# Hybrid decoder step: gate and up projections as seven block products over three token groups

## What is computed

```
x  = x + concat(A, B) @ w_out                       # output projection, 1024 -> 1024
h2 = RMSNorm(x)
g, u = split(h2 @ w_ffn_in)                         # 1024 -> 2 x 2816
gc = conv_b + conv over 3 tokens of g               # per column
x  = x + (silu(gc) * u) @ w_down                    # 2816 -> 1024
```

## Time and profile before

| | us |
|---|---|
| median of three runs | 2675.08 |
| lowest and highest run | 2668.12, 2677.18 |
| span of the profiled execution (first to last instruction) | 2668.3 |
| TensorE matmul busy | 2510.4 (94%) |
| TensorE weight load busy | 2220.7 (83%) |
| VectorE busy | 1310.5 (49%) |
| ScalarE busy | 739.9 (28%) |
| GpSimd busy | 207.2 (8%) |
| mean granted TensorE clock | 0.964 of 2.4 GHz |

### The profile page before, as it was taken

The page is one execution under the profiler, slowest core; times in us unless marked ns, Lnnn a source line. Parts: engine busy times, 40 slices in busy tenths (PEclk is TensorE's granted clock), DMA queues, the critical chain, the costliest instruction groups (busy, mean ns, idle before and its releaser), DMA issues.

```text
span 2668.3 us, 36833 instructions
## 1 busy us (share of the span) xinstructions
PE 2510.4 (94%) x13536; PEld 2220.7 (83%) x13536; DVE 1310.5 (49%) x2357; ACT 739.9 (28%) x1460; POOL 207.2 (8%) x234
## 2 busy tenths in 40 slices
PE   5999978999996799689999999999999999999998
PEld 4888857999994687578888888888999999999997
DVE  3666634666665444234444444444444444444444
ACT  2444423333331222132222222221322222222221
POOL 2223210222221000000000000000000000000000
PEclk9999968999996899899999999999999999999999
DMA  7222202111111567641111111114611111111111
GB/s 272 91 103 83 81 15 80 60 50 52 55 36 26 188 212 258 203 134 48 53 49 47 47 47 47 47 51 164 199 40 41 46 47 47 45 42 39 47 32 71
DMA packets 189315, 219.87 MB, mean 82 GB/s; under 512 B 20310, under 2 KB 152742, under 8 KB 187180
## 3 DMA queue, kind: packets, MB, share of 16 engines
q1 hardware_dynamic: 188928, 218.84, 25.1%
q10 hardware_dynamic: 288, 0.07, 0.0%
q0 software_dynamic: 32, 0.07, 0.0%
HBM read 156.77 MB, written 63.13 MB: 82 GB/s over the span
## 4 chain that ended last, share of the span: by engine, by line
PE 57%; DVE 0%; DMA 0%; issue 0%; ACT 0%; SPq 0%; DVEq 0%
PE ffn_bank L109 19%; PE ffn_bank L111 19%; PE ffn_bank L110 19%; DMA ffn_stage<-in_w_ffn_in_dram 0%; DVE ffn_stage L2383 0%; PE ffn_bank L2167 0%; DVE ffn_w_lo L2337 0%; DVE ffn_w_lo L2266 0%; ACT ffn_w_hi L2229 0%; DVE ffn_raw L2314 0%; SPq L2066 0%; DVEq L1978 0%; DVEq L77 0%
## 5 line engine op out<-in xcount | busy, mean ns | idle before, releaser
L109 PE MATMUL ffn_bank<-late_h,ffn_w_hi 128*128 128x512 f32 (+2 forms) x1760 | 619.4, 352 | 18.5 <-DVE ffn_w_lo L2337 16.5
L111 PE MATMUL ffn_bank<-late_h,ffn_w_lo 128*128 128x512 f32 (+2 forms) x1760 | 619.0, 352 | 0.0
L110 PE MATMUL ffn_bank<-late_h,ffn_w_hi 128*128 128x512 f32 (+2 forms) x1760 | 618.8, 352 | 0.0
L109 PEld LDWEIGHTS ffn_bank<-late_h,ffn_w_hi 128*128 128x128 f32 x1760 | 331.1, 188 | 47.7 <-DVE ffn_w_lo L2337 16.7
L2329 DVE TENSOR_TENSOR ffn_acc<-ffn_bank,ffn_acc 128x512 f32<-128x512 f32 (+1 forms) x374 | 257.9, 690 | 203.8 <-PE ffn_bank L111 203.8
L110 PEld LDWEIGHTS ffn_bank<-late_h,ffn_w_hi 128*128 128x128 f32 x1760 | 331.1, 188 | 28.1
L111 PEld LDWEIGHTS ffn_bank<-late_h,ffn_w_lo 128*128 128x128 f32 x1760 | 330.9, 188 | 27.8
L2303 DVE SCALAR_TENSOR_TENSOR ffn_t<-ffn_gp,ffn_cc,ffn_t 128x512 f32<-128x512 f32 (+2 forms) x220 | 142.0, 645 | 342.3 <-ACT ffn_t L2208 338.4
L109 PE MATMUL ffn_bank<-ffn_d_hi,ffn_act_hi 128*128 128x512 f32 (+1 forms) x748 | 291.4, 390 | 4.0 <-issue 4.0
L110 PE MATMUL ffn_bank<-ffn_d_lo,ffn_act_hi 128*128 128x512 f32 (+1 forms) x748 | 291.3, 389 | 0.0
L111 PE MATMUL ffn_bank<-ffn_d_hi,ffn_act_lo 128*128 128x512 f32 (+1 forms) x748 | 291.1, 389 | 0.0
(11 more groups left out here) (302 smaller groups left out, 3590.0 us busy)
## 6 DMA issues: line engine op xcount, KB each, us to landing
ffn_stage<-in_w_ffn_in_dram SPq DMA_DIRECT2D x88, 512.0 KB, 3.8
ffn_stage<-in_w_down_dram SPq DMA_DIRECT2D x44, 512.0 KB, 3.4
ml_hh<-h_parts SPq DMA_DIRECT2D x16, 1024.0 KB, 4.8
att_x<-in_x_prompt_dram SPq DMA_DIRECT2D x16, 512.0 KB, 3.5
h_parts<-att_h_hi SPq DMA_DIRECT2D x16, 512.0 KB, 2.7
h_parts<-att_h_lo SPq DMA_DIRECT2D x16, 512.0 KB, 3.4
out_o<-mixed SPq DMA_DIRECT2D x16, 512.0 KB, 5.6
out_x<-in_x_prompt_dram SPq DMA_DIRECT2D x16, 512.0 KB, 3.9
```

The source lines that it names most:

```text
L109: nc.tensor.matmul(out, a_hi, b_hi, start=first, stop=False)
L110: nc.tensor.matmul(out, a_hi, b_lo, start=False, stop=False)
L111: return nc.tensor.matmul(out, a_lo, b_hi, start=False, stop=last)
```

## The change

h2 is stored once, in fp32, and not split in `output`. `ffn` has three groups: 768, 768 and 576 tokens (the last 64 are the sample). A group's h2 is cut in four blocks: model width in halves, tokens in halves (384, 384, 288 tokens). Gate (u = 0) and up (u = 1) of the two chunks of a round are one 2x2 block product each, done with seven block products where the plain way has eight. For these, four sums of h2 blocks are made per group (three on VectorE, one on GpSimd) and four sums of weight blocks per round and unit, on GpSimd. A block product is 4 pieces times 3 matmuls of 384 (288) columns; a unit is 84 matmuls. Three banks take the seven products; ScalarE copies two of them out, VectorE adds the others in five `combine` steps. A round is now: unit 0, the down projection of the round before, unit 1. The product silu(gate)·up moves to GpSimd (`gate`), the small copies of the convolution too. The rounds are written out, with no hardware loop. Weight loads are 1 MB each, three a round. Core of the diff:

```diff
@@ output
-            def store_h(t):
-                h_split.wait(sp, t)
-                for part, src in ((0, h_hi), (1, h_lo)):
-                    h_out.mark(sp.dma_start(h2_dram[:, part, ...
+            def store_h(t):
+                h_kept.wait(sp, t)
+                h_out.mark(sp.dma_start(h2_dram[:, 0, :, bass.ds(t.n * P, r)], cut(h_t[:, t.p, :], r)), t)
...
+        def load_first(sp, q):
+            part, half = ((0, 0), (1, 0), (1, 1), (0, 1))[q]
+            ops.load_a(sp, h2_dram, GROUPS[0], part, half)
+            if q == 0:
+                ops.load_b(sp, ins["w_ffn_in"][0], 0, 0)
@@ ffn
-GROUPS = (Group(0, 0, [(0, 512), (512, 512)], False), Group(1, SEQ // 2, [(0, 384), (384, 384), (768, 320)], True))
+GROUPS = (Group(0, 0, 768, False), Group(1, 768, 768, False), Group(2, 1536, 576, True))
+PRODUCTS = ((A11, B11, 0), (S2, T2, 1), (A12, B21, 0), (S3, T3, 1), (S1, T1, 2), (A22, T4, 1), (S4, B22, 2))
+PIECE_OF = (0, 1, 0, 2, 3, 2, 3)
...
+            def unit(G, i, u):          # TensorE
+                before = (i - 1, 5 + 3, 5 + 4, 3) if u == 0 else (i, 3, 4, 1)
+                for n, (a, b, bk) in enumerate(PRODUCTS):
+                    w_split(pe, G, i, 4 * u + PIECE_OF[n])
+                    if n == 0:
+                        w_cact(pe, G, before[0], before[3])
+                    elif n == 1:
+                        w_cdve(pe, G, before[0], before[1])
+                    elif n == 2:
+                        w_cact(pe, G, i, 2 * u)
+                    elif n == 3:
+                        w_cdve(pe, G, i, 5 * u)
+                    elif n == 4:
+                        w_cdve(pe, G, before[0], before[2])
+                    else:
+                        w_cdve(pe, G, i, 5 * u + n - 4)
+                    for c in range(KH):
+                        ... three matmuls of G.H columns
...
+            def step(i):                # VectorE, i > 0
+                    split_act(G, i - 1, 0)
+                    split_d(G, i - 1, 0)
+                    split_act(G, i - 1, 1)
+                    combine(G, i, 0, 0)
+                    split_d(G, i - 1, 1)
+                    combine(G, i, 0, 1)
+                    combine(G, i, 0, 2)
+                    combine(G, i, 0, 3)
+                    split_b(G, i, 1, 0)
+                    combine(G, i, 0, 4)
+                    tap(G, i, 0)
+                    add(G, i - 1, 0)
+                    tap(G, i, 1)
+                    for n in range(1, G.NI):
+                        add(G, i - 1, n)
+                        if n in (3, 5, 7):
+                            split_b(G, i, 1, n // 2)
+                    for s in range(5):
+                        combine(G, i, 1, s)
+                        if s < 4:
+                            split_b(G_, i_, 0, s)
...
+            def step(i):                # GpSimd
+                    gate(G, i - 1, 0)
+                    gate(G, i - 1, 1)
+                    heads(G, i)
+                    sums_b(G, i, 1)
+                    tails(G, i)
+                    sums_b(*following(G, i), 0)
...
+            def step(i):                # ScalarE, i > 0
+                    round_act(G, i - 1, 0)
+                    keep_first(G, i, 0, 0)
+                    round_act(G, i - 1, 1)
+                    keep_first(G, i, 0, 1)
+                    round_b(G, i, 1, 0)
+                    conv_head(G, i, 0)
+                    conv_head(G, i, 1)
+                    ...
```

More of the change, by code:

```diff
@@ L2017, in ffn @@
-        w_tail = at(kept_tail, lambda G: 2)
-        PIECES = 6
-        def pieces(i, last):
-            out = [(0, "w", 1, 0), (1, "w", 1, 1)]
-            if not last:
-                out += [(2, "w", 0, 0), (3, "w", 0, 1)]
-            n = len(out)
-            return out + [(n, "d", 0, 0), (n + 1, "d", 1, 0)]
-        def rounds(eng, step, first=0):
-            for i in range(first, 2):
+        w_cact = at(c_act, lambda G: 4)
+        w_cdve = at(c_dve, lambda G: 10)
+        w_summed, w_rounded, w_split = (at(s, lambda G: 8) for s in (b_summed, b_rounded, b_split))
@@ L2033, in rounds, with following @@
+        def rounds(step):
+            for i in range(NP):
                 step(i)
-            with eng.Fori(2, NP - 1) as i:
-                step(i)
-            step(NP - 1)
+        def following(G, i):
+            if i < NP - 1:
+                return G, i + 1
+            return (None, None) if G.sample else (groups[G.index + 1], 0)
         block = ctx.enter_context(nc.Block())
@@ new lines, in load_d @@
+            def load_d(G, i):
+                w_down(sp, G, i - 1, G.NI - 1)
+                sp.dma_start(d_raw[:, :].rearrange("p (x n) -> p x n", x=2),
+                             ins["w_down"][0][2 * i * P:2 * (i + 1) * P, :].rearrange("(x p) n -> p x n", p=P)).then_inc(d_in, 16)
+            def group(G):
+                def step(i):
+                    load_up(G, i)
+                    if G.index > 0 and i == 0:
+                        store_y(groups[G.index - 1])
+                        sp.wait_ge(y_out, 16 * sum(g.ntile for g in groups[:G.index]))
+                        load_acc(G)
+                    load_gate(G, i)
+                    load_d(G, i)
@@ L2171, in _ @@
+            def group(G):
+                def step(i):
+                    unit(G, i, 0)
+                    if i > 0:
+                        project_down(G, i - 1)
+                    unit(G, i, 1)
+                rounds(step)
+                project_down(G, NP - 1, rows=G.sample)
             for G in groups:
@@ new lines, in sum_a @@
+            def sum_a(G, n):
+                out, x, y, op = ((S1, None, A22, ALU.add), (S2, S1, A11, ALU.subtract), (S4, A12, S2, ALU.subtract))[n]
+                if n == 0:
+                    for landed in ops.a_in:
+                        dve.wait_ge(landed, 16 * (G.index + 1))
+                else:
+                    dve.wait_ge(a_summed, 3 * G.index + n)
+                x = ops.a21(G.H) if x is None else ops.a(ops.a_raw, x, G.H)
+                nc.vector.tensor_tensor(ops.a(ops.a_raw, out, G.H), x, ops.a(ops.a_raw, y, G.H), op).then_inc(a_summed, 1)
```

718 lines of the change are left out of this document (391 added, 327 removed).

## The result

The changed kernel takes 2612.5 us (median of 4 runs, 2611.2 to 2613.1) against 2672.5 of the kernel before on the same chip (2668.1 to 2677.2): ratio 0.977, 95% interval 0.976 to 0.979, 60 us less. The forecast was 2644 us, 31 less. The profiled execution took 2612.75 us with a span of 2611.0; its span is 57.3 shorter than that of before, and the forecast for the span was 2637.

A forecast was written before the change was run, and what follows sets the result against it. It took TensorE, through the number and width of ffn's matmuls, as the bound. Its terms summed to −31 against the 2668.3 us span, giving 2637; with 7 us carried over, 2644 us, range 2580 to 2690.

The forecast's parts named there:

- matmuls: In ffn, gate and up matmuls fall from 999 to 886 us, with the down projection unchanged: −113 us.
- output stage: In output, smaller loads ahead shorten the four tiles, −14 us, and the last tile saves a split and store, −2.
- start to the first product: At the start of ffn, the first splits wait for four weight sums sharing the port: +8 us.
- steady stops before product 3: In steady rounds, VectorE and GpSimd excluding each other delay the combine: 1.5 us twenty times, 2.0 ten times, +50.
- first unit and first rounds: In each group's first round, product 1 of unit 1 waits for a split behind taps: +3.7 three times, +11 us.
- group ends: The last down projection waits for gate, round and split, then runs some matmuls at 1.2 GHz: +27 us.
- new group, late: In the new group, late split_a and the next weight load behind six 512 KB loads: +5 us.
- end: After the last down matmul, row transposes lie between the down items, so the tail shortens: −3 us.
- Rival A: The queues absorb the shared port: steady stops 0, start +2, group ends +18; 2577 us, chance 0.18.

The follow-up runs named there:

- the three runs: Changed kernel with each h2 tile stored twice in output, each piece ahead loaded twice, or both: 2612.2, 2609.8 and 2620.4 us.
- the best version: Changed kernel, w_down splits later, first rounds reordered, first weight sums and last gates on VectorE, GpSimd waiting for splits at start and group ends: 2588.9 us.

## Why the prediction was right and wrong

The causes named were there: matmuls −113, a late start, stops with a fall of the clock at the group ends, lengthened splits beside the gates, steps of 0.173 and 0.133. By its own terms, forecast and measured in the two profiles:

| term | forecast | measured |
|---|---|---|
| matmuls | −113 | −113 |
| output stage | −16 | −14 (four tiles −18.8, the two behind them +3.5, the last −2.3, ahead of the first store +4) |
| start to the first product | +8 | +7.5 |
| steady stops before product 3 | **+50** | **+15** (0.32 x 20 + 0.87 x 10: stops of 0.24 and 0.80, and 0.08 more in the step behind each) |
| first unit and first rounds | +11 | +18 |
| group ends | +27 | +26 |
| new group, late | +5 | +3 |
| end | −3 | −2.5 |
| sum | −31 | −60; the spans differ by 57, and 3 are not placed |

**The failed step is "I take 1.5 ... I take 2.0 ... Twenty rounds x 1.5 + ten x 2.0 = +50".** In the round shown above, with T = 1404.57, the gates end at T+3.1 (forecast T+3.8), split_act(0) at T+3.9 (T+4.6), split_d(0) at T+5.05 (T+5.8), split_act(1) at T+5.9 (T+6.8), the combine at T+6.4 (T+7.3). The error enters with the gates. Their record starts at 1403.48, inside a split that ends at 1404.44; from there the first needs 1.40, where the second, which nothing blocks, takes 1.85. I had charged 1.8 and 2.0, scaled from the 128x512 row, with no credit for what a blocked operation has behind it when it is released. The rest of the chain keeps the 0.7, gains another 0.2 in overlaps of neighbours (each starts some 0.07 to 0.1 before the last record's end), and lands 0.2 after the deadline in place of 1.1. On top I had added 0.4 for the weight sum getting in front; it comes at 1409.85, too late for harm in groups 0 and 1, and with the sums left out the steady rounds are no shorter. In group 2 the combine ends at T+5.45 where I had T+6.3, and the 0.5 for late taps did not come. The two runs that push the chain by one split show how sharp the edge is: +46 and +41 us for what I had at +50. The mechanism was right and sat exactly at its threshold; the size was read off a walk with an error as large as its result. Rival A named 2577, about as far below the result as the forecast lay above it. Its outcome is nearly there in groups 0 and 1 (0.32 us a round), but not its mechanism: the splits are lengthened, one more of them costs twice its length, and 9 us are paid in group 2.

**First unit and first rounds, +18 for +11.** The three stops are 3.3, 3.3 and 3.2 (3.7 forecast), but I had charged no clock behind them: 1.6 us each. The before kernel's stop of 2.1 at 1165.70 is gone. The stop of 5.1 behind the very first product, for `split_a(1)` queued behind four weight splits, I had not listed.

**Group ends.** Stops of 7.0, 9.5 and 5.9 for 9.5, 9.5 and 7.0; some fourteen matmuls at 1.2 GHz behind the first two for ten to twelve, 2.9 us each for 1.7, and 2.6 behind the third. The errors cancel, so the +26 for +27 is luck.

**Output.** I expected one of the four tiles to cost as before; none does, and they save 18.8 of 19. But the tiles behind them take 3.5 us more than before, and the way to the first store takes 4 us more, in code that hardly differs and takes 47 to 51 us in the profiles at hand. That the sum comes near the forecast is luck in part. The saving was forecast for the load's size alone; the three runs show that the smaller loads or the single store are each enough for the tiles to keep near their pace, and that half of the loss comes back when both are taken away.

**Median and span.** I carried 7 us of distance between span and median over; it is 1.5 in the changed kernel. That is 5.5 of the 31.5 us missed; the span makes 26.

## What to carry to other kernels

Where two engines exclude each other, the cost lies in what the order of both queues puts side by side, not in either's busy share: here the same splits cost +41, 0 or −12 us by their place, and making GpSimd wait for VectorE's last splits at the start and group ends was part of the best version (not run by itself). Before crediting an experiment with a few us, compare the stage that it changes: here the stages ahead of it move by 5 us between profiles of the same code. When a walk along a chain ends within a microsecond of its deadline, forecast both outcomes and their prices, for one split more or less decides 40 us. Before taking a stop away, walk the next wait behind it; three splits put ahead uncovered a longer one. And look at rounds that differ from their neighbours: here a load that took 0.3 us longer stood before each round that lost 2.4.
